# Twenty modulation pieces of a two-layer trunk on one core: fp32 matmuls replaced by two bf16 passes over halved words

## The reference, cut to what matters

```
silu_c = jax.nn.silu(c)
silu_cc = jax.nn.silu(c_ctx)
for layer in range(DEPTH):
    m_l = [m[:, None, :] for m in jnp.split(silu_c @ ada_w[layer] + ada_b[layer], 6, axis=-1)]
    m_c = jnp.split(silu_cc @ ada_w[layer] + ada_b[layer], 6, axis=-1)
    h_l = rmsnorm(x, norm_mix_g[layer]) * (1 + m_l[1]) + m_l[0]
    h_c = rmsnorm(ctx, norm_mix_g[layer]) * (1 + m_c[1]) + m_c[0]
    p_l = split_projection(h_l, w_in[layer])
    ...
    x = x + m_l[2] * (jnp.concatenate([a_l, b_l, c_l], axis=-1) @ w_out[layer])
    h2 = rmsnorm(x, norm_ffn_g[layer]) * (1 + m_l[4]) + m_l[3]
    x = x + m_l[5] * channel_mixer(h2, layer, ffn_w1, ffn_w3, ffn_w2, moe_router, moe_w1, moe_w3, moe_w2)
```

## Time and profile before

| | |
|---|---|
| median of 3 runs | 1839.96 us (1839.65 to 1841.42) |
| profiled execution, its span | 1838.2 us, 1.8 us under the median of the runs; no time of its own beside the span is given for it |
| TensorE busy | 1769.7 us, 96% of the span |
| VectorE, ScalarE, GpSimd busy | 1151.5 us (63%), 368.6 us (20%), 82.9 us (5%) |
| DMA | 408.7 MB, 222 GB/s over the span |
| mean granted TensorE clock | 0.998 |
| L454, the pieces' matmuls | 384 records of 0.592 us (two for each fp32 matmul) |

### The profile page before, as it was taken

One profiled execution on the slowest core, in us unless ns is written; L12 is line 12 of the kernel. 1 busy time (PEld: TensorE's weight loads), 2 busy tenths in 40 slices (PEclk: granted clock), 3 DMA queues, 4 the chain that ended last, 5 costly groups with the idle time before them and its releaser, 6 DMA issues.

```text
span 1838.2 us, 34033 instructions
## 1 busy us (share of the span) xinstructions
PE 1769.7 (96%) x14950; PEld 1114.3 (61%) x15001; DVE 1151.5 (63%) x1385; ACT 368.6 (20%) x671; POOL 82.9 (5%) x76
## 2 busy tenths in 40 slices
PE   6999999989999999999999978999999999999998
PEld 2434556674544444445465644878696878778695
DVE  1240176896433323214224696999999999999998
ACT  1101155242422222112013432201101010000000
POOL 0033000020000000000330001000000000000000
PEclk9999999999999999999999999999999999999999
DMA  9832200002445454230221017699999999999994
GB/s 371 309 138 69 92 1 29 18 24 98 174 188 206 183 206 160 94 113 3 89 92 69 1 47 281 255 417 409 418 416 415 418 412 419 413 418 410 412 416 194
DMA packets 98842, 408.72 MB, mean 222 GB/s; under 512 B 14008, under 2 KB 20856, under 8 KB 84368
## 3 DMA queue, kind: packets, MB, share of 16 engines
q1 hardware_dynamic: 96504, 405.54, 56.0%
q10 hardware_dynamic: 2200, 1.08, 0.2%
HBM read 405.55 MB, written 1.05 MB: 221 GB/s over the span
## 4 chain that ended last, share of the span: by engine, by line
PE 79%; DVE 10%; DMA 4%; issue 3%; ACT 2%; PEld 1%; ACTq 0%; PEldq 0%; DVEq 0%; SPq 0%; POOL 0%; POOLq 0%
PE PS L1548 12%; PE PS L1924 10%; PE PS L710 9%; PE PS L708 8%; PE PS L1506 6%; PE PS L1898 5%; PE PS L1900 5%; PE PS L1901 5%; DMA ARENA<-in_moe_w 3%; DVE ARENA L2020 2%; PE PS L454 2%; PE PS L1412 2%; PE PS L1274 2%; DVE ARENA L908 2%; DVE ARENA L905 1%
## 5 line engine op out<-in xcount | busy, mean ns | idle before, releaser
L2020 DVE TENSOR_TENSOR ARENA<-ARENA 128x2816 bf16<-128x2816 f32 (+2 forms) x184 | 567.3, 3122 | 23.1 <-DMA ARENA<-in_moe_w 22.6
L1898 PE MATMUL PS<-ARENA 128*128 128x96 bf16 x2816 | 378.6, 209 | 5.8 <-DVE ARENA L2020 3.0
L1900 PE MATMUL PS<-ARENA 128*128 128x96 bf16 x2816 | 378.4, 209 | 1.7 <-issue 1.7
L1901 PE MATMUL PS<-ARENA 128*128 128x96 bf16 x2816 | 378.3, 206 | 0.4 <-issue 0.2
L1900 PEld LDWEIGHTS PS<-ARENA 128*128 128x128 bf16 x2816 | 354.7, 126 | 8.8 <-issue 8.6
L1898 PEld LDWEIGHTS PS<-ARENA 128*128 128x128 bf16 x2816 | 346.3, 123 | 11.8 <-issue 7.5
L1901 PEld LDWEIGHTS PS<-ARENA 128*128 128x128 bf16 x2816 | 298.4, 106 | 2.5 <-issue 2.4
L710 PE MATMUL PS<-ARENA 128*128 128x512 f32 (+1 forms) x608 | 236.9, 530 | 1.3 <-DVE ARENA L623 1.3
L1924 PE MATMUL PS<-ARENA 128*96 128x512 bf16 x960 | 216.1, 384 | 0.4 <-DVE ARENA L2020 0.4
L1548 PE MATMUL PS<-ARENA 128*128 128x512 bf16 x960 | 213.5, 379 | 1.7 <-issue 0.6
L1924 PEld LDWEIGHTS PS<-ARENA 128*96 128x96 bf16 x960 | 116.2, 122 | 93.7 <-issue 0.8
(11 more groups left out here) (242 smaller groups left out, 1704.4 us busy)
## 6 DMA issues: line engine op xcount, KB each, us to landing
ARENA<-in_moe_w SPq DMA_DIRECT2D x128, 1408.0 KB, 13.9
ARENA<-in_moe_w SPq DMA_DIRECT2D x48, 1536.0 KB, 16.0
ARENA<-in_ada_w SPq DMA_DIRECT2D x24, 2048.0 KB, 10.1
ARENA<-in_ffn_w SPq DMA_DIRECT2D x15, 2048.0 KB, 7.8
ARENA<-in_w_in SPq DMA_DIRECT2D x11, 2048.0 KB, 7.9
ARENA<-in_moe_w SPq DMA_DIRECT2D x16, 1024.0 KB, 16.0
ARENA<-in_w_in SPq DMA_DIRECT2D x6, 1024.0 KB, 7.0
ARENA<-in_w_out SPq DMA_DIRECT2D x8, 512.0 KB, 4.5
```

The source lines that it names most:

```text
L1898: pe.matmul(out, hi[:, h][:, f], HEH[:, k, :], start=k == 0 and b % 4 == 0, stop=False, skip_group_check=True)
L1900: pe.matmul(out, hi[:, h][:, f], HEL[:, k, :], start=False, stop=False, skip_group_check=True)
L1901: mm = pe.matmul(out, lo[:, h][:, f], HEH[:, k, :], start=False, stop=k == KC - 1, skip_group_check=True)
L2020: dve.tensor_tensor(WLO[q % NSLOT][:, 0:n], RAW[q % NSLOT][:, 0:n], WHI[q % NSLOT][:, 0:n], ALU.subtract).then_inc(S("m_lo"), 1)
```

## The change

The pieces of layer 0 from 4 on and all of layer 1, twenty in all, are multiplied in two bf16 passes. The upper 16 bits of each fp32 weight serve as its high part where they stand, read with a stride of two 2-byte elements. VectorE writes the low part, the weight less its high part, over the lower 16 bits of the same words (`dve_ada_halve`). A strip now has four rows in use in place of two: silu of the two vectors, rounded to bf16, and what the rounding left (`dve_silu_parts`). Both passes use this strip, so all four partial products add up in four rows, which the selectors `sel` and `sel8` sum. Each of the twenty pieces becomes 16 bf16 matmuls that wait for the semaphore `ada_halved`. The step semaphores of three VectorE routines become one. Layer 0's pieces 0 to 3 stay in fp32.

```diff
-            sel[32 * g + r, r] = 1
-            sel8[32 * g + r, 2 * g + r] = 1
+            sel[[32 * g + r, 32 * g + 2 + r], r] = 1
+            sel8[[32 * g + r, 32 * g + 2 + r], 2 * g + r] = 1
...
+        SCP = BYTES[:, 1024:1536].bitcast(BF16).rearrange("p (k c) -> p k c", c=32)
...
+        def ada_halves(v):
+            v = v.rearrange("p k n -> p (k n)").bitcast(BF16).rearrange("p (k n two) -> p k n two", n=2048, two=2)
+            return v[:, :, :, 1], v[:, :, :, 0]
+
+        def ada_halved(L, j):
+            return 12 * L + j - 4 + 2
+
+        def dve_ada_halve(dve, L, j):
+            raw = raw_full(dve, ("ada", L, j))
+            hi, lo = ada_halves(raw)
+            dve.tensor_tensor(lo, ada_view(raw), hi, ALU.subtract).then_inc(S("ada_halved"), 1)
+
+        def dve_silu_parts(dve):
+            dve.wait_ge(S("sc_ready"), 1)
+            dve.wait_ge(S("filled"), 3)
+            dve.tensor_copy(SCP[:, :, 0:2], SC[:, :, 0:2]).then_inc(S("filled"), 1)
+            dve.wait_ge(S("filled"), 4)
+            dve.tensor_tensor(SCP[:, :, 2:4], SC[:, :, 0:2], SCP[:, :, 0:2], ALU.subtract).then_inc(S("ada_halved"), 1)
+
         def pe_ada_mm(pe, L, j):
             i, kk = divmod(j, 4)
-            w = ada_view(raw_full(pe, ("ada", L, j)))
+            whole = 12 * L + j < 4
             ps = B(ADA_ACC)
+            if whole:
+                parts_of, c = [ada_view(raw_full(pe, ("ada", L, j)))], SC
+            else:
+                pe.wait_ge(S("ada_halved"), ada_halved(L, j))
+                parts_of, c = ada_halves(items["ada", L, j]["raw"]), SCP
...
             for n in range(2):
-                for g in range(4):
-                    mm = pe.matmul(ps[32 * g:32 * g + 32, :], SC[:, 2 * kk + n, :], w[:, n, 512 * g:512 * g + 512],
-                                   start=kk == 0 and n == 0, stop=kk == 3 and n == 1)
+                for w in parts_of:
+                    for g in range(4):
+                        mm = pe.matmul(ps[32 * g:32 * g + 32, :], c[:, 2 * kk + n, :], w[:, n, 512 * g:512 * g + 512],
+                                       start=kk == 0 and n == 0 and w is parts_of[0],
+                                       stop=kk == 3 and n == 1 and w is parts_of[-1])
...
-                rows = slice(32 * g, 32 * g + 2)
+                rows = slice(32 * g, 32 * g + 4)
...
+        ADA_HALVED_AT = {1: (4,), 2: (5,), 4: (6,), 5: (7,)}
...
         def dve_proj_first(dve, L):
             for n in range(2 * NT):
+                if L == 0:
+                    for j in ADA_HALVED_AT.get(n, ()):
+                        dve_ada_halve(dve, 0, j)
...
             dve_qk(dve, L)
+            if L == 0:
+                for j in range(8, 12):
+                    dve_ada_halve(dve, 0, j)
...
         def dve_mix(dve, L):
             dve_norm_first(dve, L)
+            if L == 0:
+                dve_silu_parts(dve)
             dve_proj_first(dve, L)
...
                     if c == 1:
                         dve_split(dve, SPLIT_ITEMS[SPLIT_ITEMS.index(key) + 1])
+                    if chunk + 1 in ADA_CHUNKS:
+                        dve_ada_halve(dve, 1, ADA_CHUNKS[chunk + 1])
...
             dve.memset(NEGH[:, :], -0.5).then_inc(S("filled"), 1)
+            dve.memset(SCP[:, :, :], 0.0).then_inc(S("filled"), 1)
```

More of the change, by code:

```diff
@@ L400, in trunk @@
         ENG = ("pe", "act", "dve", "pool")
+        dve_steps = [0]
         stage_count = {e: 0 for e in ENG}
@@ L1708, in dve_route @@
         def dve_route(dve):
-            step = [0]
             def then(ins):
-                step[0] += 1
-                ins.then_inc(S("r_step"), 1)
-                dve.wait_ge(S("r_step"), step[0])
+                dve_steps[0] += 1
+                ins.then_inc(S("dve_step"), 1)
+                dve.wait_ge(S("dve_step"), dve_steps[0])
             def low_rows(j):
@@ L2064, in dve_moe_last @@
         def dve_moe_last(dve):
[L2066 to L2070, removed]
+            base = dve_steps[0]
+            dve.drain().then_inc(S("dve_step"), 1)
+            dve.wait_ge(S("dve_step"), base + 1)
+            dve.tensor_tensor(Y, Y, gate(1, 1, 1).unsqueeze(1).to_broadcast([P, 2, D]), ALU.mult).then_inc(S("dve_step"), 1)
+            dve.wait_ge(S("dve_step"), base + 2)
+            dve.tensor_tensor(X[:, 2:4, :], X[:, 2:4, :], Y, ALU.add).then_inc(S("dve_step"), 1)
             dve.wait_ge(S("y_last"), 1)
@@ L2075, in dve_moe_last @@
                                   ALU.mult).then_inc(S("y_last_gated"), 1)
-            dve.wait_ge(S("y_step"), 3)
+            dve.wait_ge(S("dve_step"), base + 3)
             for j, (x, h) in enumerate(LAST_PARTS):
@@ L2102, in dve_setup @@
         def dve_setup(dve):
-            step = [0]
             def then(ins):
-                step[0] += 1
-                ins.then_inc(S("setup_step"), 1)
-                dve.wait_ge(S("setup_step"), step[0])
+                dve_steps[0] += 1
+                ins.then_inc(S("dve_step"), 1)
+                dve.wait_ge(S("dve_step"), dve_steps[0])
             dve.wait_ge(S("vecs_copied"), 1)
```

## The result

The changed kernel takes **1939.94 us** (median of 4 runs, 1937.18 to 1941.0), the kernel before on the same chip 1840.69 us (1839.65 to 1842.61): a ratio of **1.0536, with a 95% interval of 1.0521 to 1.055**. The profiled execution took 1941.0 us, its span is 1939.2 us and its mean granted TensorE clock 0.971. 1924.6 us was forecast.

The account below looks back on a forecast made before the run. TensorE, busy 96% of the span, was taken as the bound. Waits of 52.1 and 30.9 plus 20.4 low clock less 18.8 gain made 84.6 us on 1838.2; with 1.8 for the median, 1924.6 us, range 1896 to 1948.

Parts of the forecast that it names:

- What is taken off TensorE: Modulation pieces in layer 0 and the FFN: 0.91 us each instead of 1.85, a gain of 18.8 us over twenty.
- What is put on VectorE: Twenty halvings of 4.42 us each; TensorE waits for some, losing 52.1 us in layer 0 and 30.9 in the FFN.
- The clock: TensorE's clock falls to 1.2 GHz behind twelve waits over 2 us, 1.7 us each, 20.4 us in all.
- The small things: Selectors, one more memset, renamed semaphores and GpSimd's rotation beside the halvings: no cost expected.
- Strips that do not run side by side (1): Rival at the pieces' matmuls: bf16 strips or strided reads do not overlap, 51 us more, 1976 us; chance 0.08.
- a halving at twice the time (2): Rival on VectorE: strided output doubles the halving's time, 53 us more, 1978 us; chance 0.05.
- A clock that holds (3): Rival on TensorE: the clock holds through the short waits, 18.7 us less, 1906 us; chance 0.17.
- absorbed (4): Rival at the expert stage's start: the slip is taken up there, 1821 us if all of it; chance 0.02.

Follow-up runs that it names:

- The filling experiment: Changed kernel with 24, 24 and 168 unread matmuls put ahead of TensorE's waits for pieces 6, 7 and 8 of layer 0; 1934.75 us.
- the last two versions above: Changed kernel with halvings re-timed and each piece's load given its own time, then piece 9's load time 28.5 for 30: 1837.38 us, 1832.29 us.
- two of the cures tried here: Changed kernel with FFN halvings ahead of the weight split, 1923.22 us; changed kernel with all halvings placed by when TensorE wants them, 1848.15 us.

## Why the prediction was right, and where it was off

The direction and the mechanism held. 1924.6 was forecast and 1939.94 came, 15.3 us more, inside the range.

| term | forecast | measured |
|---|---|---|
| pieces shorter | 18.8 (0.94 each) | 16.6 (0.83 each) |
| layer 0: waits of 4, 6, 7, 8 | 4.5, 5.3, 5.3, 37.0 | 4.45, 5.47, 5.47, 37.13 |
| FFN: waits of 0, 1, 2, 4 | 5.3, 4.6, 3.7, 4.9 | 5.38, 4.60, 4.03, 5.48 |
| FFN: waits of 7, 8, 9, 10 | 3.7, 3.5, 2.6, 2.2 | 4.01, 3.80, 3.07, 1.48 |
| FFN: waits of 6, 11 | 0.2, 0.2 | 0.58, 0.75 |
| sum of waits | 83.0 | 85.7 |
| low clock | 20.4 (12 x 1.7) | 32.1 (31.8 piece by piece) |
| sum | 84.6 | 101.2 |

- **What is taken off TensorE.** Measured 1.02 us for a piece, against my 0.91. Four strips of bf16 run 3.47 / 1.02 = 3.4 times as fast as one after another, not 3.8 as in fp32. The Trainium skill (TensorE: Matmul & The Clock Gate, section on the measured speedup against the span model) has 3.07 times for four row tiles, by which the estimate for a piece is 1.13 us. The measured 1.02 us lies between that and mine. Whether it is the bf16 or the stride that costs the 0.1 us was not tried. The kernel without halvings, 15.5 us faster than the one before, bears the term out.
- **What is put on VectorE.** The waits, gone through piece by piece, came out within 0.8 us each, 2.7 us too low in all. Which pieces wait and which do not was right for all twenty. The small error is mostly one number: the halvings that TensorE waited for took 4.67 to 5.08 us and not the 4.42 of a split. Layer 1 back in fp32 (-42.0) and piece 8 moved (-38.8) show the two halves of this term apart.
- **The clock.** This step was mis-sized: 32.1 us against 20.4. The term of the sum was 12 waits at 1.7 us, priced from a single idle, behind which the granted clock was 0.59 for 3.2 us and 0.80 for 2.0. Behind the wait at 54.48 it stayed at 0.50 for 9.6 us, and the eleven waits that it followed cost 1.6 to 4.6 us each, 2.9 on average. What sets how long the clock stays low behind one wait is open. The filling experiment shows that it is a cost of the idle time itself: with three waits filled, 7.7 us came back.
- **The small things.** I had costed GpSimd's rotation at nothing and it did cost TensorE nothing, but not because it was undisturbed (below).
- **The rivals.** Strips that do not run side by side (1) and a halving at twice the time (2) are out: 1.02 us, and at most 5.9. A clock that holds (3) is out but for waits of 1.5 us and less; between 1.5 and 3 us it went either way (in the last two versions above a wait of 2.23 us was followed by a stretch at 0.50, and one of 2.72 us by none). Nothing was absorbed (4): the expert stage moved by the whole slip.
- **Sum.** Waits 2.7 more, clock 11.7 more, pieces 2.2 less gain: 16.6 us, which is the 101.2 measured to the expert stage against 84.6. All three errors have the same sign, so none hid another, and the number fell inside the range because the range allowed for a dearer clock.

## What to carry to other kernels

Work put on a free engine costs what stands ahead of it in that engine's order when the busy engine asks for it: write down for each such step when it is wanted and when the one ahead of it is over, since 100 us of free VectorE time made 86 us of waits in one order and 6 us in another. Add to such a wait what the low clock behind it costs: here 1.6 to 4.6 us behind each of the eleven waits of 3 us and more, 2.9 on average. And when a step is moved earlier, look for what it pushes back, on its own engine and in the in-order queue of loads, because two of the cures tried here brought a new wait of 3 to 5 us with them.

## What the runs showed that I had not expected

**The halving slows down a little when TensorE works.** In the kernel after, the halvings during which TensorE stood idle all but the first 0.3 us or less took 4.67 or 4.68 us; those beside which it worked for 1 us or more took 4.97 us and more, even the one at 597.33, which took 4.98 us although TensorE stood idle for the last 4.03. That TensorE's work is the cause is shown by the filling alone (4.67 to 5.00 and 5.03). Which resource the two share no run tells. A split, fp32 less bf16 on as many elements, took 4.42 us with TensorE at work. A halving differs from it in reading the bf16 operand, and in writing its result, at every second 2-byte place, and in writing over its own input; which of these costs the rest was not tried.

**GpSimd stands still beside a halving.** Timeline of GpSimd, kernel after:

```profile
160.09 10.52 POOL L893 TENSOR_TENSOR ARENA<-ARENA,K 128x256 f32<-128x256 f32 x2 [8.41 <-DVE ARENA L870]
```

The same pair took 1.40 us before. It lies beside the two halvings from 159.93 on, which took 10.13 us together, and ends about when they do. With piece 8 moved, the first operation of GpSimd's powers fell beside a halving that ran from 149.35 for 5.05 us (timeline of GpSimd, that experiment):

```profile
149.54 4.94 POOL L878 TENSOR_SCALAR STAT<-STAT 128x64 f32<-128x64 f32 x1 [104.57 <-DVE STAT L856]
```

Before, this operation took 0.26 us. The Trainium skill (SBUF — State Buffer, section "Who interferes with whom") says that a VectorE instruction with both inputs in SBUF contends with a GpSimd instruction that reads SBUF; the two rows agree, and they show that the small one waits about as long as the whole large one. It goes the other way as well: in the kernel after, the halvings at 175.93 and 186.40, beside GpSimd's rotation, took 5.45 and 5.90 us. GpSimd's busy time went from 82.9 to 101.4 us. No wait of TensorE for GpSimd or for what follows it grew, since the rotation is wanted much later; in a kernel whose TensorE waits for GpSimd it would be the first thing to look at.
